# The last block of a fused transformer kernel: where its state tables, its sums of squares, its query norms and its picks are computed

## The reference

```python
h = h + 0.5 * swiglu(rms_norm(h, ffn2_norm[l]), ffn2_w_gu[l], ffn2_w_down[l])   # l = 1, the last layer
x = rms_norm(h, final_norm)[:, 16:]
# second block, 512 positions
h = _rms(x, norm1_g)
u, q, k, v, qi, ki, wi, gates = split(h @ w_in)
y_ssm = _s5_branch(u, A_re, A_im, log_dt, B_re, ...)        # diagonal complex state space, 32 groups x 64 states
q = _rms(q.reshape(bsz, L, 8, 64), q_norm_g)                # norm over each head's 64 columns
k = _rms(k, k_norm_g); ki = _rms(ki, idx_k_norm_g)
iscore = sum_h relu(qi_h . ki) * wi_h                       # an index score for each pair of positions
idx = top_k(iscore, 128)                                    # the 128 best keys of each query
logits = (q . k[idx]) * 64 ** -0.5;  o = softmax(logits) @ v[idx]
merged = sigmoid(g_ssm) * (y_ssm @ w_proj_ssm) + sigmoid(g_att) * (o @ w_proj_attn)
x = x + merged @ w_out;  x = x + swiglu(_rms(x, norm2_g))
```

## Time and profile before

| | us |
|---|---|
| median of 3 runs | 3425.16 |
| lowest, highest | 3420.05, 3425.9 |
| the profiled execution's own time | 3419.99 |
| its span | 3418.1 |
| PE busy | 3280.1 (96%) |
| DVE busy | 1392.2 (41%) |
| POOL busy | 1278.9 (37%) |
| ACT busy | 1053.0 (31%) |
| PE in the chain that ended last | 66%, and 23% "issue" |

### The profile page before, as it was taken

The page is one execution under the profiler, slowest core; times in us unless marked ns, Lnnn a source line. Parts: engine busy times, 40 slices in busy tenths (PEclk is TensorE's granted clock), DMA queues, the critical chain, the costliest instruction groups (busy, mean ns, idle before and its releaser), DMA issues.

```text
span 3418.1 us, 54419 instructions
## 1 busy us (share of the span) xinstructions
PE 3280.1 (96%) x21472; PEld 2961.2 (87%) x21472; DVE 1392.2 (41%) x2138; ACT 1053.0 (31%) x1485; POOL 1278.9 (37%) x589
## 2 busy tenths in 40 slices
PE   8999989999999999999989998999997988999999
PEld 8999988898999999999989887788775676778887
DVE  4121443477521123121353487522336766552212
ACT  4222433322332224222343322332233433242222
POOL 3444432122444434434432122444436351144443
PEclk9999999999999999999999999999999988999999
DMA  4333321133332323333322133333232432233333
GB/s 131 92 88 91 89 62 50 47 92 106 99 93 87 92 86 93 92 92 89 90 64 62 41 93 111 114 92 96 88 87 65 96 77 91 74 100 98 93 93 98
DMA packets 544842, 298.63 MB, mean 87 GB/s; under 512 B 23281, under 2 KB 528625, under 8 KB 544561
## 3 DMA queue, kind: packets, MB, share of 16 engines
q1 hardware_dynamic: 514128, 258.77, 26.6%
q10 hardware_dynamic: 30560, 37.72, 3.4%
HBM read 278.36 MB, written 16.91 MB: 86 GB/s over the span
## 4 chain that ended last, share of the span: by engine, by line
PE 66%; issue 23%; POOL 6%; DVE 4%; ACT 1%; ACTq 0%; DMA 0%; POOLq 0%; DVEq 0%; SPq 0%
PE pair L575 37%; PE pair L573 27%; POOL wl L474 5%; DVE xl L1413 0%; PE aux L599 0%; DVE negt L1888 0%; DVE tmp L1412 0%; PE aux L930 0%; DVE top L1887 0%; PE aux L931 0%; PE pair L877 0%; ACT xh L987 0%; DVE tmp L1860 0%; PE aux L655 0%; ACT tmp L986 0%
## 5 line engine op out<-in xcount | busy, mean ns | idle before, releaser
L474 POOL TENSOR_TENSOR wl<-raw,wh 128x1024 fp32r<-128x1024 f32 (+4 forms) x549 | 1222.6, 2229 | 2098.8 <-ACT wh L973 2098.3
L973 ACT ACTIVATE wh<-raw 128x1024 fp32r<-128x1024 f32 (+4 forms) x549 | 528.1, 964 | 475.6 <-DMA raw<-ffn_w_down 160.5
L1399 DVE TENSOR_TENSOR tmp<-pair,rstd 128x528 f32<-128x528 f32 (+1 forms) x222 | 155.7, 702 | 812.5 <-PE pair L575 500.1
L575 PE MATMUL pair<-xh,wh 128*128 128x264 f32 x3072 | 462.1, 290 | 17.3 <-DVE xl L1413 12.2
L575 PE MATMUL pair<-xh,wl 128*128 128x264 f32 x3072 | 447.0, 285 | 0.9 <-POOL wl L474 0.9
L575 PE MATMUL pair<-xl,wh 128*128 128x264 f32 x3072 | 447.3, 285 | 0.0
L575 PEld LDWEIGHTS pair<-xh,wh 128*128 128x128 f32 x3072 | 404.4, 190 | 25.3 <-ACT wh L973 9.3
L575 PEld LDWEIGHTS pair<-xh,wl 128*128 128x128 f32 x3072 | 403.4, 189 | 1.2 <-POOL wl L474 1.2
L575 PEld LDWEIGHTS pair<-xl,wh 128*128 128x128 f32 x3072 | 403.9, 189 | 0.0
L1423 DVE SCALAR_TENSOR_TENSOR hT<-pair,hT 128x528 f32 (+3 forms) x144 | 100.7, 700 | 474.0 <-PE pair L575 273.0
L573 PE MATMUL pair<-xh,wh 128*128 128x512 f32 x1064 | 289.5, 405 | 3.7 <-issue 2.2
(11 more groups left out here) (320 smaller groups left out, 3973.6 us busy)
## 6 DMA issues: line engine op xcount, KB each, us to landing
raw<-ffn_w_gu SPq DMA_DIRECT2D x176, 512.0 KB, 3.8
raw<-w_in SPq DMA_DIRECT2D x103, 512.0 KB, 3.9
raw<-ffn_w_down SPq DMA_DIRECT2D x64, 512.0 KB, 3.8
raw<-ffn_w_down SPq DMA_DIRECT2D x32, 384.0 KB, 3.3
raw<-w_out SPq DMA_DIRECT2D x24, 512.0 KB, 3.8
raw<-w_ffn_gate SPq DMA_DIRECT2D x22, 512.0 KB, 3.7
raw<-w_ffn_up SPq DMA_DIRECT2D x22, 512.0 KB, 3.8
gate_scratch<-gst ACTq DMA_DIRECT2D x32, 256.0 KB, 2.3
```

Source lines behind the costliest of these rows:

```text
L474: nc.gpsimd.tensor_tensor(wl[:, k % SPL, 0:n], raw[:, k % SPL, 0:n], wh[:, k % SPL, 0:n].bitcast(F32), ALU.subtract).then_inc(S["split_don ...
L575: mm = nc.tensor.matmul(pp[:, h, 0:th], wk, x[:, kk, t0 + h * th:t0 + (h + 1) * th], start=first, stop=last)
L973: nc.scalar.activation(wh[:, k % SPL, 0:n], raw[:, k % SPL, 0:n], ACT.Copy).then_inc(S["split_hi"], 1)
L1399: v.tensor_tensor(halves(dst, th), psum_pair(0 if alone else k, th), halves(scale, th), ALU.mult).then_inc(S["evacuated"], 1)
```

## The change

Nothing of the result changes. What moves:

1. `discretise` is cut into nine pieces and placed beside down units of segments 0 and 1; none stays beside the last eight down units. ACT's four functions for it move with them.
2. The last eight down units get `residual_twice`. ACT rounds first and squares after; DVE adds tile m to `hT` before it turns to tile m-1; the sums have a semaphore of their own (`sq_ok`) and the four squares have two buffers each.
3. `tables(0)` runs on POOL one instruction after each split of the last segment's gate and up units, `tables(1)` one after each split of U_IN2, `tables(2)` and `tables(3)` between gate splits, with waits for `mk_done` and `y_done` inside the generator.
4. The query norms are no longer applied to the queries. Their sums come per row (`q_sums`: four matmuls of 2 columns in place of one of 512); one root and one reciprocal of 128x32 (`rq`) give a factor for each row and head. In attention DVE multiplies each row maximum by it (a 128x1 instruction more per step) and the exponential takes it as its scale. The query gain goes into the key gain.
5. Picks: 28 before attention in place of 34. One gate unit moves from the state loop into slot 0 of attention step 0; the last two U_PROJ2 units move behind the last values. The D-skip products (line 1984) are one per step (n = 5 to 8) in place of two (n = 7, 8).

```diff
-        LATE = EARLY + 8
+        LATE = EARLY + 7
+            if n == 0:
+                return 8, 3
...
+            return (2, 1) if n >= PROJ_AT else (0, 0)
 # POOL
+                for g, nf in enumerate(SEGS):
+                    if beside is not None and g == len(SEGS) - 1:
+                        for j in range(2 * nf):
+                            split(l, k + j, KD)
+                            next(beside, None)
...
             for j in range(13):
                 split(None, U_IN2 + j, KD)
-                if 1 <= j < 4:
-                    next(ahead_of[0])
-                if j in (6, 8, 10):
-                    next(ahead_of[1])
+                if j >= 1:
+                    more(1, 1)
...
-                if b < 2:
-                    pool.wait_ge(S["y_done"], b + 1)
-                    for _ in tables(b + 2):
-                        pass
+            more(2, 3)
+            split(None, U_GATE2 + EARLY + 3, KD)
+            more(2, 4)
+            split(None, U_GATE2 + EARLY + 4, KD)
+            more(3, 9)
 # PE
+            def q_sums(j):
+                pe.wait_ge(S["n2_sq"], j + 3)
...
+                for i, (st, sz) in enumerate(TT2):
+                    c = HEADS * i + 2 * j
+                    mm = nc.tensor.matmul(bank[2][:, c:c + 2], tm(SQ, SEQ)[:, st:st + sz], bd64[:, 0:P:64], start=True, stop=True)
 # ACT
+            def residual_twice(l, ub, nrm, gain, T):
+                for m in range(KD):
+                    act.wait_ge(S["evacuated"], U(l, ub + m) + 1 + PAIRS)
+                    hm = hT[:, m, T1 - T:T1]
+                    nc.scalar.activation(xh[:, m, 0:T], hm, ACT.Copy, scale=gain(m)).then_inc(S["norm_act"], 1)
+                    if m >= 2:
+                        act.wait_ge(S["sq_ok"], m - 1)
+                    nc.scalar.activation(tm(SQ2[m % 2], T), hm, ACT.Square)
+                    nc.scalar.activation(tm((SG, US)[m % 2], T), hm, ACT.Square, scale=vec[:, V_GAIN + 48 + m:V_GAIN + 49 + m]).then_inc(S["sq_act"], 1)
+                    ahead(l, ub + m)
 # DVE
+                def tile(m):
+                    dve.wait_ge(S["norm_act"], t0 + m + 1)
+                    v.scalar_tensor_tensor(xl[:, m, 0:T], hT[:, m, T1 - T:T1], gain(m), xh[:, m, 0:T].bitcast(F32), ALU.mult, ALU.subtract).then_inc(S["x_ready"], 1)
+                    dve.wait_ge(S["sq_act"], m + 1)
...
+                for m in range(KD):
+                    add_residual(l, ub + m, m, factor, T)
+                    if m >= 1:
+                        tile(m - 1)
+                tile(KD - 1)
...
+                if (g, m) in ((0, 3), (0, 4), (0, 6), (0, 7), (1, 1), (1, 5), (1, 6), (1, 7)):
                     next(pieces)
...
+                    if scale is not None:
+                        step(top)
+                        top = v.tensor_tensor(nmx[0:sz, n:n + 1], nmx[0:sz, n:n + 1], scale[0:sz, n:n + 1], ALU.mult)
...
-                pick(2)
-                gates(EARLY + 2 * b + 1, EARLY + 2 * b + 2)
-                pick(4)
+                    pick(3)
+                    gates(EARLY + 2 * b + 1, EARLY + 2 * b + 2)
+                    pick(1)
+                else:
+                    pick(2)
```

More of the change, by code:

```diff
@@ L1453, in ffn @@
                     k += 2 * nf
[L1454 to L1456 removed]
+                    if g < len(SEGS) - 1 and hook is not None:
+                        for m in range(KD):
+                            add_residual(l, k + m, m, factor, T)
+                            hook(g, m)
+                    elif g < len(SEGS) - 1:
                         with dve.Fori(0, KD // 4) as i:
@@ L1495, in merged, with attention @@
                 lo(KD - 1)
-            def attention(A, out_to, between=None, before=None):
+            def attention(A, out_to, between=None, before=None, scale=None, tail=None):
                 tt, sm = A.tt, A.sem
```

198 lines of the change are left out of this document (110 added, 88 removed).

## The result

The changed kernel takes **3382.0 us** (3380.3 to 3384.0, 4 runs) beside 3425.5 for the kernel before; the ratio is 0.9872, 95% interval 0.9852 to 0.9892. The gain is 43.5 us where 58 were forecast (3425.2 - 3367).

The account below looks back on a forecast made before the run. PE was taken as the bound, unfed between 2541 and 3002 us with DVE behind it. Terms -6.5 - 23 - 7 - 16 - 6 - 5 + 6.5 + 0 = -57 us gave 3363, median 3367 us, range 3346 to 3396.

Parts of the forecast that it names:

- (a): `discretise` pieces at a segment's end: PE's wait near 2434 us goes, -6.5 us (bounds -3 and -7).
- (b): Last eight down units to the sums: DVE keeps close to PE's pace, -23 us (bounds -17 and -27.8).
- (c): In-projection: query norms leave PE, ACT and DVE, and waits go, -7 us (bounds -3 and -9).
- (d): State loop: POOL's table order and fewer picks shorten waits and low-clock time, -16 us (bounds -7 and -26).
- (e): Attention's start: fewer picks and a gate unit before the transposes remove PE's wait, -6 us (bounds -4 and -6.7).
- (f): Attention's steps: -5 us from spread D-skip products, against +6.5 for late picks and the row-maximum product, clock included.
- (g): Attention's end: two projection units moved behind the last values, 0 us (bounds -3 and +4).
- A: Rival: POOL's table work contending with DVE takes gain back, leaving -25.5 us, about 3397; chance 0.12.
- B: Rival: waits caused the low clock, so PE stays at 2.4 GHz without them, -83.5 us, about 3340; chance 0.05.
- C: Rival: POOL holds the row-maximum product in attention's 32 steps, up to 77 us, 20 us slower, about 3444; chance 0.03.
- D: Rival: nothing gained; ACT's last-tile chain sets the sums' wait and loop waits only move, about 3422; chance 0.02.

Follow-up runs that it names:

- e9: Changed kernel with the query norms applied to the queries again, no factor on row maximum or exponential; 3389.0 us, ratio 0.9879.
- e1: Changed kernel with three of attention's pick rounds moved ahead of gate unit 9's taking out, none left in steps 18 to 20; 3380.3 us.
- e4: Changed kernel with 22 useless matmuls of 512 columns added on PE in attention steps 18 to 23; 3378.1 us, ratio 0.9843.
- e10: Kernel before with only the `discretise` pieces moved and the new `residual_twice` order with its own semaphore; 3408.7 us, ratio 0.9941.
- e3: Changed kernel with POOL's `tables(1)` instructions behind splits 3 to 8 and 10 to 12 of U_IN2, not 1 to 9; 3376.0 us, ratio 0.9852.
- e12: Changed kernel with the edits of e1 and e3 plus 45 useless matmuls in the state loop and attention steps 18 to 23; 3365.5 us, ratio 0.9825.

## Why the prediction was right, and where its steps were off

The direction, the order of the terms and the range were right; the gain came out 15 us smaller than forecast. Its own sum of 57 makes 3368 from the median of 3425.2, put at 3367. By its steps:

- **(a), -6.5, measured -6.5.** The wait of the earlier trace rows is gone, and parts 1 and 2 alone give the same (-7.1). That DVE's late taking out and not ACT was the last thing is read from the trace of before: ACT rounds three units ahead, and the `wh` that ends at 2439.84, just ahead of PE's start, is of a unit whose weights were loaded only after 2434.6, when the unit four before it ended. No run moves DVE's pieces and leaves ACT's functions.
- **(b), -23, measured -21.1.** DVE's lag was taken as 1.5 us and is 0: first to last matmul of the eight units is 33.2 us, PE's own pace of 4.17 a unit. The chain behind it, that of the earlier trace rows, was taken as 8 us between 5.5 and 12 (0.9 + 10.4 + 1.4 is 12.7) and is 11.8, near the worst case, since POOL had four instructions in a row there. The rule "one of DVE's for each of POOL's" was right (2.6, 2.6 and 2.4 us for the 2.6 assumed); the mistake was to take the middle where the queue of POOL could be counted out.
- **(c), -7, measured -1.5.** The waits at the query norms went as forecast (-4.2). Taken back was 2.6 us at unit 8, 1.0 of wait and 1.6 of clock: the bound of -3 named `tables(1)` meeting DVE in nine units, but as a general slowing, and not at the one instruction that frees ACT's buffer. The 1.5 us for smaller sums didn't show: a query unit with its sums takes 6.45 us, with the matmul of 512 it took 6.42, so the four matmuls of 2 columns cost PE as much. The bound of -3 was too narrow.
- **(d), -16, measured -14.0.** POOL's wait is gone (-5.7), L959's fell from 4.1 to 1.8, the state's stayed (5.6, now 5.8 in four), the clock's low share from 27 to 13 us of the loop. That is 7.8 us of waits where 10.2 were forecast, and by half of the low time 7 of clock where 6 were. The shares can't be told apart by undoing: POOL's old order alone takes back 11.2, six picks alone 12.9. Each lengthens the same chain from scan to state, and the clock goes with it.
- **(e), -6, measured -5.2.** First score to first transposes are 9.9 us with the gate unit of 5.56 in them, 9.55 without before. The gate unit itself ran half at the lower clock.
- **(f), -5 + 6.5, measured -1.7 + 9.4.** The failed step, and with (c) the larger part of what is missing. The part ahead of exponential 18 gave 1.7 of 5: e9 shows that the row scale costs some 4 us there, where the forecast counted it in six later steps alone. The forecast, from the earlier trace rows, priced the picks (+3.8) and the product (+1.5) as DVE's time. At 2.4 GHz the +1.5 fits e1, for the product and the dearer exponential together. But the changed kernel's profile had these steps at 1.2 GHz, where PE needs 4.0 us a step: at least 6.3 of the 9.4 us are the clock's (e4), and e10 took 34.1 us at that clock without picks or product. The picks' +3.8 is at most 2.5 by e4 and e1. The bound of +15 covered it, but for DVE's time and not PE's.
- **(g), 0, measured -0.6;** moving the units back costs 1.0, some 7 us at the lower clock included.

One reading ahead of the sum was right on a row that doesn't show it. That what reads PSUM isn't held was taken from L1423 at 2439.06, but POOL's split began only at 2439.91, after both had started. In the changed kernel the same addition (L1469) starts at 2574.01 in the middle of a split (2573.45 to 2575.86) and takes 0.69 us.

The rivals: A named contention as what takes the gain back, and in (b) and (c) it does, for 6 us (e3 gets 3.4 and 2.6 of it back, 1.6 by the clock), not 31. B, that the lower clock is a result of PE's idleness, has e4 and e12 for it, in whose profiled executions the clock held with filler in steps 18 to 25; as a forecast it was wrong, since the waits that are gone didn't keep the clock up. C and D are refuted. The page "ScalarE: Activation LUTs" of the Trainium skill (What ACT_TABLE_LOAD costs) has 93 ns for a pointer operand; the exponential went from 578 to 667 ns and by 84 to 89 ns at the other widths, so the trace agrees. L1490, held for POOL's full length, agrees with the page "SBUF — State Buffer" of the Trainium skill (Who interferes with whom), and so does L1941 (1.37 us for 0.35): the same section counts `tensor_scalar` among the operations that can take the shared ports in a two-port mode, with a single tensor input, which I hadn't weighed in term (c).

**What stays open.** Why the clock falls in steps 18 to 25 in one execution and not in another with the same instructions there (each kernel has one execution with a trace). It held in the profiled executions of before and of e1, and with filler in e4 and e12; it fell in all others, e10 among them, whose steps are those of the kernel before. Picks, product, scale and the place of the units are each ruled out as the sole cause; that PE has less than its full work there is common to all. Filler as what holds it rests on two profiled executions, and two without filler held as well. The profiled execution of before happened to be one in which it held and that of after one in which it fell, so the +9.4 us of the table by stage is in part the choice of executions (its mean clock is 0.981, and 0.975 to 0.980 in the 29 of before that the experiments were compared with); the medians, 43.5 apart, lean less on it. Whether the loop's variation (92.6 to 98.7 us with the same instructions) is the same effect wasn't tried by itself.

## What to carry to other kernels

Where an instruction of DVE on two SBUF tensors is in the chain that PE waits for, count POOL's queue at that moment, instruction by instruction: each costs its full length (here 2.4 to 2.7 us), and moving two of them away gave 3.4 us with DVE's own work unchanged. Judge a stretch in which PE isn't fed in full by its granted clock first: here eight steps mostly at 1.2 GHz took 34.4 us without picks and 33.2 with them, so what was saved on DVE wasn't seen. Work for PE placed in it, even useless work, cost nothing here. And compare single profiles stage by stage, since two executions of one kernel differ by more (up to 21 us) than most of the parts under study.

## What the runs showed of the hardware that I had not expected

- The same instructions in the same order took 23.8 us at a granted clock of 1.00 and 34.1 us at 0.65 (steps 18 to 25 of before and of e10).
- Useless matmuls cost nothing: with 45 of 512 columns, 10.4 us at their pitch, the kernel takes 3365.5 us, without them 3370.7 (ratios 0.9825 and 0.9829), and its executions lie within 7.4 us in place of 17.4.
- Of two 128x1 products in a row behind the maximum the first took 0.42 us in the mean and the second 0.16: POOL's hold fell on the first and never on the one right behind it.
- Not only instructions on two tensors were held by POOL: a TENSOR_SCALAR on one SBUF tensor with a 128x1 operand took 1.37 us for 0.35 (L1941), and by it PE stood 1.0 us longer.
- A wait longer by 1.0 us cost 2.6: in after the unit behind it ran at a granted clock of 0.72 and took 1.6 us more than in e4, which has the same wait and kept 1.00.
